# The feed-forward part of a hybrid decoder block, walked in pairs of column blocks with four accumulators open at once

## What is computed

```python
    h = h + (g_attn * y_attn + g_ssm * y_ssm) @ w_out[layer]
    u = rms_norm(h, mlp_norm_w[layer]) @ w_up[layer]        # w_up   2048 x 8192
    h = h + jnp.square(jax.nn.relu(u)) @ w_down[layer]      # w_down 8192 x 2048
```

## Time and profile before

| | |
|---|---|
| median of 3 runs | 1998.27 us (1998.1 to 1998.66) |
| span of the profiled execution | 1996.6 us; its own launch time isn't printed, the median lies 1.7 us above the span |
| PE busy | 1991.1 us, 100%, 9106 matmuls |
| DVE busy | 1302.9 us, 65% |
| ACT busy | 1128.0 us, 56% |
| feed-forward part on PE | from 1295.7 to 1993.4 us |
| HBM read | 382.46 MB, 193 GB/s over the span |

### The profile page before, as it was taken

How to read it: one execution, slowest core, us unless ns; L and a number is a source line. 1 busy time by engine, 2 the same in 40 slices (tenths; PEclk the granted TensorE clock), 3 DMA queues, 4 the chain that set the end, 5 groups by cost and what they waited for, 6 DMA issues and landing times.

```text
span 1996.6 us, 25655 instructions
## 1 busy us (share of the span) xinstructions
PE 1991.1 (100%) x9106; PEld 1647.8 (83%) x9106; DVE 1302.9 (65%) x1511; ACT 1128.0 (56%) x1301; POOL 198.7 (10%) x191
## 2 busy tenths in 40 slices
PE   9999999999999999999999999999999999999999
PEld 8888888888887888888888888888888888888887
DVE  5777777777888777776675665656555555654554
ACT  6666666667776555556764444555445435534542
POOL 2110120112231211110000000010000000000000
PEclk9999999999999999999999999999999999999999
DMA  7787887889997666666996667767667666766775
GB/s 248 205 204 203 215 201 202 222 231 237 245 231 217 193 197 194 195 190 189 233 241 204 200 208 237 219 190 232 197 189 211 223 195 190 234 199 181 218 221 162
DMA packets 332464, 419.52 MB, mean 210 GB/s; under 512 B 147264, under 2 KB 147712, under 8 KB 332112
## 3 DMA queue, kind: packets, MB, share of 16 engines
q1 hardware_dynamic: 331456, 415.23, 73.0%
q10 hardware_dynamic: 448, 2.24, 0.3%
q0 software_dynamic: 464, 0.77, 0.2%
HBM read 382.46 MB, written 2.16 MB: 193 GB/s over the span
## 4 chain that ended last, share of the span: by engine, by line
PE 98%; ACT 1%; DVE 0%; DMA 0%; issue 0%; SPq 0%; DVEq 0%; ACTq 0%
PE ps L676 32%; PE ps L677 31%; PE ps L678 31%; PE ps L855 1%; PE ps L624 1%; PE ps L842 0%; DMA f_half<-r_half 0%; PE ps L688 0%; PE ps L727 0%; PE ps L750 0%; PE ps L876 0%; ACT whi L987 0%; PE ps L724 0%; ACT r_half L1479 0%; PE ps L752 0%
## 5 line engine op out<-in xcount | busy, mean ns | idle before, releaser
L1518 DVE TENSOR_TENSOR wlo<-raw,whi 128x1024 fp32r<-128x1024 f32 x703 | 886.9, 1269 | 600.8 <-ACT whi L987 598.6
L987 ACT ACTIVATE whi<-raw 128x1024 fp32r<-128x1024 f32 x703 | 738.3, 1057 | 602.0 <-PE ps L678 578.8
L676 PE MATMUL ps<-whi,xT_hi 128*128 128x512 f32 x1268 | 498.3, 393 | 0.0
L678 PE MATMUL ps<-whi,xT_lo 128*128 128x512 f32 x1268 | 493.8, 389 | 0.0
L677 PE MATMUL ps<-wlo,xT_hi 128*128 128x512 f32 x1268 | 493.5, 389 | 0.0
L678 PEld LDWEIGHTS ps<-whi,xT_lo 128*128 128x128 f32 x1268 | 238.0, 188 | 50.2
L676 PEld LDWEIGHTS ps<-whi,xT_hi 128*128 128x128 f32 x1268 | 238.1, 188 | 49.0 <-issue 1.4
L677 PEld LDWEIGHTS ps<-wlo,xT_hi 128*128 128x128 f32 x1268 | 238.2, 188 | 47.3
L676 PE MATMUL ps<-whi,fT_hi 128*128 128x512 f32 x512 | 199.3, 389 | 0.1
L676 PE MATMUL ps<-whi,hT_hi 128*128 128x512 f32 x512 | 199.3, 389 | 0.0
L678 PE MATMUL ps<-whi,hT_lo 128*128 128x512 f32 x512 | 199.2, 389 | 0.0
(11 more groups left out here) (290 smaller groups left out, 1989.8 us busy)
## 6 DMA issues: line engine op xcount, KB each, us to landing
raw<-in_w_in SPq DMA_DIRECT2D x319, 512.0 KB, 4.3
raw<-in_w_up SPq DMA_DIRECT2D x128, 512.0 KB, 4.2
raw<-in_w_down SPq DMA_DIRECT2D x128, 512.0 KB, 4.3
raw<-in_w_ssm_out SPq DMA_DIRECT2D x64, 512.0 KB, 4.2
raw<-in_w_attn_out SPq DMA_DIRECT2D x32, 512.0 KB, 4.0
raw<-in_w_out SPq DMA_DIRECT2D x32, 512.0 KB, 4.4
arow<-arows SPq DMA_DIRECT2D x16, 512.0 KB, 4.9
x_in<-in_x SPq DMA_DIRECT2D x4, 512.0 KB, 8.0
```

What stands on the lines that cost most here:

```text
L676: mm(dst, xh, whi[sl][:, kk, :], start=(s == 0 and kk == 0), stop=False)
L678: last = mm(dst, xl, whi[sl][:, kk, :], start=False, stop=(s == US - 1 and kk == UK - 1))
L987: A(whi[s % SLOTS][:, :, :], raw[s % SLOTS][:, :, :], ACT.Copy).then_inc(hi_ready, 1)
L1518: V.tensor_tensor(wlo[s % SLOTS][:, :, :], raw[s % SLOTS][:, :, :], fp(whi[s % SLOTS][:, :, :]), ALU.subtract).then_inc(lo_ready, 1)
```

## The change

The 32 blocks of the feed-forward part become 16 pairs (`PAIRS`) of two neighbouring column blocks, in the same order: pairs m = 0, 1 (mod 4) are up pairs, m = 2, 3 (mod 4) down pairs. A pair is walked in eight quads of two units: row range s of the left block, then row range s of the right block. So four accumulators are open over the whole pair, banks 0 and 1 for token tile 0 (left, right), banks 6 and 7 for token tile 1, and every pair uses the same four. Only the last pair ends differently: its quads 6 and 7 take both row ranges of the left block, then both of the right block.

- **PE** waits on `c_free` at the first matmul into each bank of a pair, for the emptying of the previous pair.
- **ACT** empties an up pair at its end with one ReLU over two banks for each token tile, into `ust` (128x2048); then it squares all of it itself (POOL's and DVE's squarings are gone), and takes it apart in two halves, one quad later each. For pair 0 the two ReLUs stand before the rounding of the first quad of pair 1; for every later up pair they stand after the rounding of the second quad of the next pair.
- **DVE** makes the remainders of a quad in one instruction of 128x2048 that waits for both roundings, and empties a down pair with one addition of 128x1024 for each token tile.
- **SP** has a third buffer for raw quads (6 units in all instead of 4) and issues the two transposes of a half back to back, the ones of the second half only when those of the first have landed.
- A form with seven products (`seven`, `UP_SEVEN`, `DOWN_SEVEN`) is written too, but its lists are empty: nothing of it runs. In the same way some semaphores of the earlier parts are shared under new names, with no other order.

```diff
+QUADS = 8
+PAIRS = 16
+M0 = B_MLP * US
+UP_SEVEN = ()
+DOWN_SEVEN = ()
...
+def quads(m):
+    order = (UP_ORDER, UP_ORDER_LATE, DOWN_ORDER, DOWN_ORDER_LATE)[m % 4]
+    if m < PAIRS - 1:
+        return [(True, s) if s in seven(m) else (False, ((s, 0), (s, 1))) for s in order]
+    head = [(True, s) if s in seven(m) else (False, ((s, 0), (s, 1))) for s in order[:6]]
+    return head + [(False, ((order[6], 0), (order[7], 0))), (False, ((order[6], 1), (order[7], 1)))]
...
+        raw4 = [sb("raw4", *(("RAW", 8192 * j) if j < 2 else ("D", 12 * KB)), [P, 4, COLS]) for j in range(3)]
+        whi4 = [sb("whi4", "HI", 8192 * j, [P, 4, COLS], f32r) for j in range(2)]
+        wlo4 = [sb("wlo4", "LO", 8192 * j, [P, 4, COLS], f32r) for j in range(2)]
...
             def r_turn(n, a):
                 sp.wait_ge(r_halved, n + 1)
+                if n % 2:
+                    sp.wait_ge(r_turned, 32 * n)
+                    src, dst = r_half1[:, a, 0:NTOK, :], f_half1
...
+                            if n < 2:
+                                sp.wait_ge(lo_ready, M0 + 2 * n + i - 3)
+                            elif n > 2:
+                                sp.wait_ge(lo_ready, M0 + 2 * n + i - 5)
...
+                    if m and (m - 1) % 4 < 2 and j in TURN_AT:
+                        p = (m - 1) // 4 * 2 + (m - 1) % 4
+                        for a in range(2):
+                            r_turn(2 * p + TURN_AT.index(j), a)
+            TURN_AT = (4, 5)
...
+            C_BANK = ((0, 1), (6, 7))
...
+                def product(bank, xh, xl, wh, wl):
+                    first = not begun[bank]
...
+                    if bank in (0, 1, 6, 7) and first and m:
+                        pe.wait_ge(c_free, 2 * m - 1 if bank < 2 else 2 * m)
...
+                def classical(j, what):
+                    for i, (s, a) in enumerate(what):
+                        n = M0 + 2 * (QUADS * m + j) + i
+                        sl = n % SLOTS
+                        inputs_ready(s)
+                        pe.wait_ge(hi_ready, n + 1)
+                        pe.wait_ge(lo_ready, n + 1)
+                        for t in range(NTOK):
+                            for kk in range(UK):
+                                kt = UK * s + kk
+                                last = product(C_BANK[t][a], x_hi[:, kt, t * P:(t + 1) * P], x_lo[:, kt, t * P:(t + 1) * P],
+                                               whi[sl][:, kk, :], wlo[sl][:, kk, :])
...
+                def inputs_ready(s):
...
+                    if m % 4 == 2:
+                        pe.wait_ge(fT_lo_done, 4 * (m // 4) + s // 2 + 1)
...
+            def mlp_hi(m, j, only=None):
...
+                    for i in range(2) if only is None else only:
+                        act.wait_ge(raw_in[raw_slot(m, j, i)], raw_count(m, j, i))
+                        act.wait_ge(unit_used, n + i - SLOTS + 1)
+                        A(dst[:, 2 * i:2 * i + 2, :], src[:, 2 * i:2 * i + 2, :], ACT.Copy).then_inc(hi_ready, 1)
...
+            def relu(m):
+                for t in range(NTOK):
+                    pair = ust[:, 2 * t:2 * t + 2, :]
...
+                        act.wait_ge(unit_used, M0 + 2 * QUADS * (m + 1))
...
+                        A(pair, banks[:, 6 * t:6 * t + 2, :], ACT.Relu, scale=rstd2[:, t:t + 1]).then_inc(c_free, 1)
...
+            for m in range(PAIRS):
+                before = m - 1 if m and (m - 1) % 4 < 2 else None
+                if m == 0:
+                    mlp_hi(0, 1, only=(1,))
+                    h_hi()
+                    h_squares(3)()
+                for j in range(QUADS):
...
+                    if j == 7 and m == 0:
+                        relu(0)
+                    if (m or j) and (m, j) != (PAIRS - 1, QUADS - 1):
+                        mlp_hi(m + (j + 1) // QUADS, (j + 1) % QUADS)
+                    if before is not None:
+                        if j == 0:
+                            if before:
+                                relu(before)
+                            square(before)
+                        if j in (1, 2):
+                            r_halve(before, j - 1)
+                        if j in (3, 4):
+                            f_hi(before, j - 3)
...
+                    dve.wait_ge(hi_ready, n + 2)
+                    V.tensor_tensor(lo[:, :, :], src[:, :, :], fp(hi[:, :, :]), ALU.subtract).then_inc(lo_ready, 2)
...
+            def h_from_banks(m):
+                dve.wait_ge(unit_used, M0 + 2 * QUADS * (m + 1))
...
+                for t in range(NTOK):
+                    i = V.tensor_tensor(h_pair(m, t), banks[:, 6 * t:6 * t + 2, :].rearrange("p a n -> p (a n)"),
+                                        h_pair(m, t), ALU.add)
+                    i.then_inc(c_free, 1)
...
+                for j in range(QUADS):
+                    if before is not None and before % 4 < 2 and j in (3, 4):
+                        f_join(before, j - 3)
...
+                    if (m or j) and not (last and j == QUADS - 1):
+                        mlp_lo(m + (j + 1) // QUADS, (j + 1) % QUADS)
+                    if before is not None:
+                        if before % 4 < 2 and j in (3, 4):
+                            f_lo(before, j - 3)
...
+                    if j == 7 and not last:
+                        if m % 4 >= 2:
+                            h_from_banks(m)
```

More of the change, by code:

```diff
@@ L239, in sem @@
             return ctx.enter_context(nc.semaphore(name))
-        raw_in = [sem(f"raw_in{s}") for s in range(SLOTS)]
+        raw_in = [sem(f"raw_in{s}") for s in range(SLOTS + 2)]
         half_in = sem("half_in")
@@ L976, in _ @@
+            pe.wait_ge(set_free[0], 26)
+            for m in range(PAIRS):
+                mlp_pair(m)
         @block.scalar
@@ L1489, in mlp @@
-            def mlp(q, end=False):
-                b = B_MLP + 8 * q
-                for u in range(4):
-                    w = {7: [relu(b + u, u % 2, 4 * q + u)]}
-                    if not later(q) and u == 0:
-                        w[1] = [h_hi, h_squares(3)]
-                    if u:
-                        w[0] = [r_halve(4 * q + u - 1)]
-                        w[4] = [f_hi(4 * q + u - 1, u - 1)]
-                    steps(b + u, w)
-                steps(b + 4, {0: [r_halve(4 * q + 3)], 4: [f_hi(4 * q + 3, 3)]})
-                for d in range(1, 4):
-                    steps(b + 4 + d, last=end and d == 3)
@@ new lines, in square, with r_halve @@
+            def square(m):
+                p = m // 4 * 2 + m % 4
+                if seven(m):
+                    act.wait_ge(r_ready, p + 2 * sum(1 for i in range(m + 1) if i % 4 < 2 and seven(i)))
+                else:
+                    act.wait_ge(c_free, 2 * m + 2)
+                A(ust[:, :, :], ust[:, :, :], ACT.Square).then_inc(r_ready, 1)
+            def r_halve(m, a):
+                p = m // 4 * 2 + m % 4
+                dst = r_half1[:, :, 0:NTOK, :] if a else r_half0[:, :, :, :]
+                if a:
+                    act.wait_ge(r_halved, 2 * p + 1)
+                else:
+                    act.wait_ge(r_ready, p + 1 + 2 * sum(1 for i in range(m + 1) if i % 4 < 2 and seven(i)))
+                    if p:
+                        act.wait_ge(f_joined, 2 * p)
+                A(dst, ust[:, a:4:2, :].bitcast(u16).rearrange("p t (n a) -> p a t n", a=2), ACT.Copy).then_inc(r_halved, 1)
@@ new lines, in up_sums, with h_pair @@
+            def up_sums(m):
+                dve.wait_ge(unit_used, M0 + 2 * QUADS * (m + 1))
+                dve.wait_ge(u_done, 3 * seven_pairs_before(m) + 3)
+                for t in range(NTOK):
+                    pair = ust[:, 2 * t:2 * t + 2, :]
+                    V.tensor_tensor(pair, banks[:, 6 * t:6 * t + 2, :], pair, ALU.add).then_inc(c_free, 1)
+            def h_pair(m, t):
+                c0 = (m % 4 - 2) * 2 * COLS
+                return h[:, t, c0:c0 + 2 * COLS]
+            def h_from_banks(m):
+                dve.wait_ge(unit_used, M0 + 2 * QUADS * (m + 1))
+                if m > 3 and seven(m):
+                    dve.wait_ge(h_step, 2 * seven_downs_before(m) - 2)
+                for t in range(NTOK):
+                    i = V.tensor_tensor(h_pair(m, t), banks[:, 6 * t:6 * t + 2, :].rearrange("p a n -> p (a n)"),
+                                        h_pair(m, t), ALU.add)
+                    i.then_inc(c_free, 1)
@@ new lines, in f_join @@
+            def f_join(m, a):
+                p = m // 4 * 2 + m % 4
+                n = 2 * p + a
+                dve.wait_ge(r_turned, 32 * n + 32)
+                if n:
+                    dve.wait_ge(fT_lo_done, n)
+                src = f_half1 if a else f_half0
+                for pl in range(2):
+                    i = V.tensor_copy(halves(f_st[:, :, :].rearrange("p c t -> p (c t)"))[:, pl, :],
+                                      src[:, pl, :, :].rearrange("p (t c) l -> p c t l", t=NTOK))
+                i.then_inc(f_joined, 1)
```

556 lines of the change are left out of this document (384 added, 172 removed).

## The result

The changed kernel takes 2045.1 us (2044.4 to 2046.7, 4 runs) against 1998.18: a ratio of 1.0235, 95% interval 1.0221 to 1.025. Forecast was 2036.2, range 2030 to 2050. The direction, the places of the waits and their causes were right; 9 us of the 46.9 were missing, most of them lost to TensorE's clock.

What follows compares the result with a forecast made beforehand. The prediction took TensorE, busy all of the span, as the bound. Its five terms, 1.8 + 6.7 + 16.5 + 10.2 + 2.7 = 37.9 us, on 1998.3 gave 2036.2 us, range 2030 to 2050.

Steps and rivals of the forecast that it cites:

- What bounds the kernel: Whole kernel: TensorE is busy throughout, one matmul start every 0.2266 us; any delay of a matmul delays the end equally.
- The steady state: Inside a pair: no cost; weights take 3.65 of a quad's 5.44 us; moved squarings and third load buffer change nothing.
- Term 1: Start, third quad of pair 0: unit 4's rounding stands behind `h_hi` and the squares; 1.8 us, once.
- Term 2: End of pair 0: banks not emptied and weights not ready, ReLUs ahead of the roundings on ACT; 6.7 us, once.
- Term 3: Ends of the seven other up pairs: ReLU queued behind a rounding on ACT; 2.36 us each, 16.5 us.
- Term 4: Ends of seven down pairs that another follows: PE waits for DVE's addition of 1024; 1.46 us each, 10.2 us.
- Term 5: Clock after pair 0's long gap: one unit at half rate, 2.7 us (bounds 0 and 5.4); shorter gaps 0.
- my own rival: The clock falls at every pair end: 14 more gaps cost 2.7 us each, giving 2074 us; chance 0.06.
- late transposes: Pairs after up pairs: transposes landing over 6.2 us make PE wait; at 7 us +13, 2049 us; chance 0.12.
- Cheaper matmuls: Feed-forward matmuls: rotating over four banks could bring the step to 0.2133 us, saving 41 us: 1995; chance 0.02.
- doesn't do what it says: Pair ends: emptying comes in the pair's own shadow, PE's wait is elsewhere; within 4 us of 1998; chance 0.02.
- signs in the profile: Feed-forward part: PE idle about 35 us in 16 pieces with named releasers; clock below 1.00 only behind the long gap.

Runs made afterwards that it cites:

- the last kernel: Against the change: two sets of four banks in turn, start mended, second rounding before the ReLUs at every up pair end, pair 0's too; 1998.05 us, ratio 0.9998.
- the two sets: Against the change: pairs use two sets of four banks in turn (0, 1, 6, 7 and 2, 3, 4, 5), all else kept; 2009.4 us.
- the kernel whose waits are all short: Against the change: start, pair 0's weights before its ReLUs, and ReLUs before the second rounding at up pairs, all mended; still four banks; 2022.12 us.

## Why the prediction was right, and where it was short

**What bounds the kernel** held: PE's stream was the end of everything, the step stayed 0.2265, and each delay showed in the time in full.

**The steady state** held: no wait inside a pair in the profile of the change. The squaring on ACT, POOL's work gone and the third load buffer moved nothing. The banks and ACT's orders make up the whole loss: with two sets, the start mended and pair 0's weights first, the last kernel has none of it left. The third order, of the later up pairs, stands in that kernel as in the change; it costs only with one set.

**Terms 1 to 4** were 35.2 and measured 36.9. Term 1: 1.94 for 1.8. Term 2: 6.70 for 6.7, with errors of up to 0.06 in its parts that cancel. Term 3: 2.46 for 2.36, term 4: 1.57 for 1.46, seven of each. The 0.1 at each end is PE's restart: I took 0.04 from the earlier trace rows, while here PE starts 0.15 after DVE's addition ends (1441.90 and 1.22, to 1443.27) and 0.14 after the ReLU (1395.26 and 1.10, to 1396.50). The prices of instructions twice as long, worked out from slopes, were right: 2.29 for 2.31 (L2343), 1.10 for 1.12 (L1709), 1.22 for 1.23 (L2392).

```profile
L2343 DVE TENSOR_TENSOR wlo<-raw,whi 128x2048 fp32r<-128x2048 f32 x126 | 288.7, 2292 | 368.5 <-ACT whi L1676 368.5
L1709 ACT ACTIVATE ust<-ps,rstd 128x1024 f32<-128x1024 f32 x16 | 16.8, 1103 | 9.8 <-PE ps L1086 9.8
L2392 DVE TENSOR_TENSOR h<-ps,h 128x1024 f32<-128x1024 f32 x14 | 16.5, 1220 | 13.5 <-PE ps L1086 13.5
```
The mechanism of term 3, a rounding ahead of the ReLU, is shown by the kernel with the ReLUs first; that of term 2 by the one with pair 0's weights first; the bank reuse behind terms 3 and 4 by the two sets.

**Term 5 was the mis-sized one**, in the sentence "The gaps of 1.5 to 2.4 us are near the row: 0 for them." The waits of 2.3 us idle lie twice as high as the row of 1.13, as my own rival said of them ("gaps twice the longest"), and four of seven lowered the clock, 6.6 us. The part for the long gap, one unit or 2.7 us, measured 1.5, as the low stretch had begun within the gap. With 6.6 in place of that sentence's zero the sum would have been 2043. The waits of 1.4 behind down pairs were indeed free of it, so "near the row" was right for these. The rule of the Trainium skill that I weighed (TensorE: Matmul & The Clock Gate, "What's actually happening") was borne out at the long gap; without a length of idleness, as I weighed it, it couldn't tell which of the shorter waits cost clock. My own rival, a fall at every pair end, had 0.06: it named what was missing and went too far, with none behind the down pairs.

**The first steps after a wait** (0.07 each, 0.8 in all) were not in the sum. The missing 9 us are thus 1.7 in terms 1 to 4, 5.4 in the clock (8.1 for 2.7), 0.8 in the first steps, and 1.1 that lies outside these places: 0.3 of the span, and 0.8 by which the time grew more than the profiled span.

**The range held by luck.** What I worked out for this mechanism ended at 2044, below the measured 2045.1. The stretch up to 2050 was added for the late transposes, and these didn't happen.

**The rivals.** Late transposes: no. The landing times of the change's transposes are 3.6 us in the middle and 5.6 at most, under the 4.2 and 6.1 of the earlier trace rows (why isn't shown), and the view lists no wait of DVE's joins (L2432) for one:

```profile
L542 SPq DMA_TRANSPOSE f_half<-r_half x32: 1232/1260/2157, 1359.1 to 1966.2; - x32
L2432 DVE COPY f_st<-f_half x32: 731/755/783, 1365.0 to 1972.6; 128x1024 uint16<-128x1024 uint16 x32
...
DMA to landing us min/median/max: 3.1/3.6/5.6
```

Cheaper matmuls and "doesn't do what it says": neither, the step is unchanged and the waits stand at the places named. The forecast of signs in the profile (sixteen waits with their releasers) was met but for the low clock, which I had expected only behind the long gap, and which I named as what would prove me wrong elsewhere.

## What to carry to other kernels

When PE is the bound, the price of a group of accumulators that is emptied and taken again at once is the chain from its last matmul to the end of the first instruction that frees a bank, whatever is queued ahead of that instruction included, and PE's restart; here it could be read in advance from the rows of the old kernel to within 0.15 us for each wait. Which instruction should come first on the emptying engine depends on what PE will want first: with one set of banks the emptying, with two sets the next weights. Count a wait twice when it is long (here 2.3 us and more): once for itself, and once for the clock it may take along.

## What the runs showed of the hardware that was not expected

A single PE idle time of 2.3 us lowered TensorE's clock to 1.2 GHz in 23 of 35 cases, for some 3.4 us each, with 1.65 us of delay where it was read, whereas 86 idle times of 0.9 to 1.8 us never did. The 40 slices of the page showed a clock of 9 tenths throughout; only windows of a few microseconds behind the waits, and the mean clock of 0.995, gave it away. The spread goes with it: 2.3 us over four runs of the change, 0.6 over four of the kernel whose waits are all short, and in the kernel with four extra matmuls 2.5 us between executions at a mean clock of 0.994 and 0.996.
